# Moving the next page's transposes behind a page's first half of key products

## The chip, the cores and the metric

The kernel runs on one core of one Trainium2 chip. The metric is device microseconds of one launch, lower is better. Engines are named as in the profile: PE is TensorE, PEld its weight loads, DVE is VectorE, ACT is ScalarE, POOL is GpSimd, SP is SyncE.

## What is computed

One layer of a decoder for a prompt of 256 tokens and 8 sample sequences with a cache of 2048 positions each. Two branches (a gated delta rule and latent attention) share a normalised input, are merged by gates, and an MLP follows. The part at stake is the attention of the 8 samples over 16 cached pages each, 128 pages in all, every page 128 positions of 512 latent and 64 rope values:

```python
def mla_keys(latent, w_uk, w_uv, k_norm_nope):
    c = latent[..., :KV_LORA].astype(w_uk.dtype)
    kr = latent[..., KV_LORA:].astype(w_uk.dtype)
    kn = rms_norm((c @ w_uk).reshape(bsz, s, MLA_HEADS, NOPE_DIM), k_norm_nope)
    ...
def page_block(phys):
    kn, kr, v = mla_keys(cache_l[phys], w_uk, w_uv, k_norm_nope)
    return partial_softmax(mla_scores(qn, qr, kn, kr), v)
```

The kernel needs the product `c @ w_uk` (128 x 512 by 512 x 1024) of each page only for its sums of squares, that is for the norm of each head's key. The scores themselves come from queries that were multiplied into the latent space beforehand, four pages at a time.

## The kernel before, in words

The program has three stages: projections of prompt and sample (to about 209 us in the trace), a loop over the 128 pages (209 to 1350 us), and the gates and the MLP. All instructions are placed by hand, engine by engine; engines meet at semaphores only, and each runs its list in order. There is no scheduler.

In the loop, page n belongs to group g = n // 4 at position t = n % 4. The steps, by the names of the code:

- `transposes(n)` (PE, L1765): four 128x128 transposes of the page in `craw` into one bank of PSUM. `turned_page(n)` (ACT) copies that to `cTr` (L673) and rounds it to `cTh` (L676). `split_lo(n)` (DVE, L1079) writes the rest, `cTl = cTr - cTh`.
- `keys(n, half)` (PE, L1774 to L1776): twelve matmuls of 512 columns for each half of the key columns; it waits for `cTl` of its page. `squares(n, half)` (ACT, L682) squares the result, `norms(n, half)` (DVE, L1083) sums it by head.
- `query_products(g)` (PE, L1793 and L1795) at t = 3, `score_rows` (ACT, L692), `score_columns` (PE, L1801), `score_parts` (DVE, L1087), `maxima(g - 1)` (DVE, L1101 and L1103), `exps(g - 1)` (ACT, L698, writes `pst`), and on the next page, t = 0, `weigh(g - 2)` (PE, L1809, reads `pst`), `latent_rows` (ACT, L704), `latent_columns` (PE, L1815). At t = 2 `rope_columns` (PE, L1784) and `turned_rope` (ACT, L687). At t = 1 the DVE adds up scores and values of earlier groups.
- `beside(i)` on each engine: the delta rule runs as side work, pair of heads by pair of heads, in slots. Slot i = 2n stands before `keys(n, 0)`, slot 2n + 1 before `keys(n, 1)`. A pair takes 52 steps, k = 0 to 51, and the four pairs fill slots 6 to 213; the slots after them are empty. A step's PE part writes a bank, its DVE or ACT part reads it, and the PE part of the next step often waits for that.

Steps of the side work that the prediction names: k = 21 (ACT square root with a table load, L757), k = 22 (DVE Newton step), k = 27 (DVE writes `T_`, L1258 and L1260) and k = 28 (PE reads it, L1918), k = 49 (ACT square root with a table load, L779), k = 50 (DVE Newton step from L1175 to L1179), k = 51 (PE, L1835, reads its result).

The order on each engine within page n is before: PE `query_products` or `weigh`, `transposes(n + 1)`, `beside(2n)`, `keys(n, 0)`, the columns of that t, `beside(2n + 1)`, `keys(n, 1)`; ACT `latent_rows` or `score_rows`, `turned_page(n + 1)`, `beside(2n)`, `squares(n, 0)`, `turned_rope` or `exps`, `beside(2n + 1)`, `squares(n, 1)`; DVE `beside(2n)`, `split_lo(n + 1)`, `norms(n, 0)`, the sums of that t, `beside(2n + 1)`, `norms(n, 1)`.

Of the kernel before, what the change touches and what calls it, by code (L numbers as in the profile page):

```python
# [36 lines left out]
NT = NS * PAGES  # L37
# [101 lines left out]
def pair_slot(i):  # L139

    k = i - B_START
    return divmod(k, B_SLOTS) if 0 <= k < HP * B_SLOTS else (None, None)
# [11 lines left out]
def build(nc, I, O):  # L154
    C_in, ctx = I["consts"], ExitStack()
    with ctx:
        sems = {}

        def S(name):
            if name not in sems:  # L160
                sems[name] = ctx.enter_context(nc.semaphore(name))
            return sems[name]
# [234 lines left out]
        def wait(eng, name, value):  # L397

            if not isinstance(value, int) or value > 0:
                eng.wait_ge(S(name), value)  # L400
# [179 lines left out]
        def _(act):  # L580
# [97 lines left out]
            def squares(n, half_):  # L678
                k = 2 * n + half_
                act.wait_ge(S("half_done"), k + 1)  # L680
                wait(act, "kss_done", k - 1)
                nc.scalar.activation(ksq[:, half_], ps[:, k % 3, :], ACT.Square).then_inc(S("ksq_ready"), 1)  # L682

            def turned_rope(gg):
                act.wait_ge(S("rope_done"), gg + 1)
                wait(act, "qk_done", gg)
                nc.scalar.activation(rpT[:], ps[0:64, B_SUM, :], ACT.Copy).then_inc(S("rope_ready"), 1)  # L687

            def score_rows(gg):
                act.wait_ge(S("qk_done"), gg + 1)  # L690
                wait(act, "pvt_done", gg - 1)
                nc.scalar.activation(prows[:], ps[:, B_SCORE, :], ACT.Copy).then_inc(S("ssb_ready"), 1)  # L692
# [88 lines left out]
            def z_high(i):  # L781
                ns = NP + i
                act.wait_ge(S(f"z_landed{i % 2}"), 16 * (i // 2 + 1))
                if i >= 2:
                    act.wait_ge(S("chunk_done"), 4 * (ns - 1))
                nc.scalar.activation(wh2[:, ns % 2], wraw2[:, i % 2], ACT.Copy).then_inc(S("w_hi"), 1)

            def beside(i):
                b, k = pair_slot(i)
                if i < B_START:  # L790
                    decay_steps(i)
                elif b is not None:
                    pair_act(b, k)
                elif i == 2 * NT - 20:
                    z_high(0)
                elif i == 2 * NT - 16:
                    z_high(1)

            turned_page(0)
            for n in range(NT):  # L800
                g, t = n // 4, n % 4
                if t == 0 and g >= 2:
                    latent_rows(g - 2)
                if t == 3:
                    score_rows(g)
                if n + 1 < NT:
                    turned_page(n + 1)
                beside(2 * n)
                squares(n, 0)
                if t == 2:  # L810
                    turned_rope(g)
                if t == 3 and g >= 1:
                    exps(g - 1)
                beside(2 * n + 1)
                squares(n, 1)
# [62 lines left out]
        def _(v):  # L878
# [202 lines left out]
            def norms(n, half_):  # L1081
                v.wait_ge(S("ksq_ready"), 2 * n + half_ + 1)
                V.tensor_reduce(kss[:, n // 4 % 2, n % 4, 4 * half_:4 * half_ + 4], ksq[:, half_].rearrange("p (h d) -> p h d", h=4), AX, ALU.add).then_inc(S("kss_done"), 1)  # L1083
# [267 lines left out]
            def beside(i):  # L1351
                b, k = pair_slot(i)
                if i < B_START:
                    decay_steps(i)
                elif b is not None:
                    pair_dve(b, k)
                elif i == 2 * NT - 18:
                    z_low(0)
                elif i == 2 * NT - 14:
                    z_low(1)  # L1360

            split_lo(0)
            for n in range(NT):
                g, t = n // 4, n % 4
                beside(2 * n)
                if n + 1 < NT:
                    split_lo(n + 1)
                norms(n, 0)
                if t == 1 and g >= 1:
                    scaled(g - 1)  # L1370
                if t == 1 and g >= 2:
                    probabilities(g - 2)
                    latent_sum(g - 2)
                if t == 3:
                    score_parts(g)
                if t == 3 and g >= 1:
                    maxima(g - 1)
                beside(2 * n + 1)
                norms(n, 1)
                if t == 3:  # L1380
                    v.wait_ge(S("kss_done"), 2 * n + 2)
                    V.tensor_scalar(kss[:, g % 2], kss[:, g % 2], 1.0 / 128, EPS, ALU.mult, ALU.add).then_inc(S("ms_ready"), 1)  # L1382
# [154 lines left out]
            for g in range(2):  # L1537
                for u in range(8):
                    n = 8 * g + u + 2
# [13 lines left out]
        def _(pe):  # L1553
# [207 lines left out]
            def transposes(n):  # L1761
                pe.wait_ge(S(f"pages_landed{n // 4 % 3}"), 64 * (n // RING) + 64)
                wait(pe, "ct_raw", n)
                for c in range(4):
                    k = nc.tensor.transpose(trp[:, c, :], craw[:, n % RING, P * c:P * c + P], ident)  # L1765
                k.then_inc(S("tr_done"), 1)
# [31 lines left out]
            def score_columns(gg):  # L1798
                pe.wait_ge(S("ssb_ready"), gg + 1)
                for t in range(4):  # L1800
                    k = nc.tensor.transpose(stp[:, t, :], prows[:, P * t:P * t + P], ident)  # L1801
                k.then_inc(S("st_done"), 1)
# [180 lines left out]
            def beside(i):  # L1983
                b, k = pair_slot(i)
                if i == 5:
                    pe.wait_ge(S("g_ready"), 1)
                    pe.wait_ge(S("beta_ready"), 1)
                    p_ = begin_a("bg")
                    for n in range(2):
                        j = nc.tensor.transpose(p_[:, 64 * n:64 * n + 64], rw[:, CH * n:CH * n + CH], ident[0:64, 0:64])  # L1990
                    a_done(j)
                if b is not None:
                    pair_pe(b, k)

            transposes(0)
            for n in range(NT):
                g, t = n // 4, n % 4
                if t == 3:
                    query_products(g)
                if t == 0 and g >= 2:  # L2000
                    weigh(g - 2)
                if n + 1 < NT:
                    transposes(n + 1)
                beside(2 * n)
                keys(n, 0)
                if t == 0 and g >= 2:
                    latent_columns(g - 2)
                if t == 2:
                    rope_columns(g)
                if t == 3:  # L2010
                    score_columns(g)
                beside(2 * n + 1)
                keys(n, 1)

# [135 lines left out]
```

## Time and profile before

| | us |
|---|---|
| median of 3 runs | 1740.8 (1740.1 to 1743.41) |
| the profiled execution, its own time | 1745.99 |
| its span, first to last instruction | 1744.2 |
| PE busy in the span | 1674.2 |
| DVE busy | 898.7 |
| ACT busy | 638.4 |

The profiled execution is one run; its own time is 1.8 us above its span and 5.2 us above the median. PE is the engine that is nearly always busy, and its clock is granted in full in nearly all of the loop. A row of the trace reads: start in us from the span's start, length in us, engine, line, operation, names written and read; an idle stretch before it and what ended it stand in brackets.

### The profile page before, as it was taken

What the parts mean: (1) busy time and instruction counts of PE and PEld (TensorE: products, weight loads), DVE (VectorE), ACT (ScalarE), POOL (GpSimd) and SP (SyncE); (2) the same over time, 40 slices, a digit from 0 to 9 for tenths busy, and PEclk for the clock granted to TensorE, in tenths of its full rate; (3) what the DMA queues carried; (4) which work ended last, traced back from release to release, by engine and by line L of the source; (5) the groups of instructions that cost most, each with busy time, mean ns of one, the idle gap of its engine ahead of it and who ended that gap; (6) DMA issues with size and microseconds to landing.
All of it is one profiled execution on the core that took longest, in us unless ns stands there. A gap on an engine that the chain in (4) does not pass through costs nothing.

```text
span 1744.2 us, 26102 instructions
## 1 busy us (share of the span) xinstructions
PE 1674.2 (96%) x10164; PEld 1371.4 (79%) x10164; DVE 898.7 (52%) x1650; ACT 638.4 (37%) x954; POOL 213.5 (12%) x111
## 2 busy tenths in 40 slices
PE   6889899999999999999999999999999878999998
PEld 5865788687787787787877787876777778999998
DVE  5865444544455545455444555444333344677733
ACT  3221244533344433445333335234353323334431
POOL 0020011112111111211111211112121100000000
PEclk9995799999999999999999999999999988999999
DMA  7301132111232101331102310003110524555551
GB/s 241 97 1 55 50 82 64 40 29 39 73 88 65 28 28 30 96 87 53 28 28 57 103 41 28 28 28 115 43 55 1 175 91 169 170 169 176 186 177 66
DMA packets 110916, 138.68 MB, mean 80 GB/s; under 512 B 13584, under 2 KB 60208, under 8 KB 110664
## 3 DMA queue, kind: packets, MB, share of 16 engines
q1 hardware_dynamic: 106022, 134.43, 25.1%
q10 hardware_dynamic: 4602, 2.05, 0.5%
q8 instruction: 79, 1.29, 0.3%
q0 software_dynamic: 176, 0.61, 0.1%
q14 instruction: 37, 0.30, 0.1%
HBM read 130.52 MB, written 6.74 MB: 79 GB/s over the span
## 4 chain that ended last, share of the span: by engine, by line
PE 88%; DVE 7%; issue 2%; ACT 1%; ACTq 1%; POOL 0%; DVEq 0%; POOLq 0%
PE ps L1774 14%; PE ps L1776 13%; PE ps L1775 13%; PE ps L2070 5%; PE ps L2071 5%; PE ps L2072 5%; PE ps L1765 4%; PE ps L1793 2%; PE ps L1809 2%; PE ps L1860 1%; PE ps L1859 1%; PE ps L1861 1%; PE ps L1835 1%; PE ps L1926 1%; PE ps L1918 1%
## 5 line engine op out<-in xcount | busy, mean ns | idle before, releaser
L1774 PE MATMUL ps<-ukh,cTh 128*128 128x512 f32 x1024 | 425.7, 416 | 0.3 <-DVE cTl L1079 0.3
L1083 DVE TENSOR_REDUCE kss<-ksq 128x4 f32<-128x512 f32 x256 | 175.4, 685 | 447.8 <-ACT ksq L682 447.1
L1776 PE MATMUL ps<-ukh,cTl 128*128 128x512 f32 x1024 | 404.7, 395 | 0.0
L1775 PE MATMUL ps<-ukl,cTh 128*128 128x512 f32 x1024 | 404.0, 395 | 0.0
L682 ACT ACTIVATE ksq<-ps 128x512 f32<-128x512 f32 x256 | 152.7, 596 | 565.1 <-PE ps L1776 565.0
L1774 PEld LDWEIGHTS ps<-ukh,cTh 128*128 128x128 f32 x1024 | 194.7, 190 | 58.9 <-issue 24.2
L571 POOL TENSOR_TENSOR rk<-kss,mhalf 128x32 f32<-128x32 f32 x32 | 178.8, 5587 | 507.1 <-DVE kss L1382 507.1
L1776 PEld LDWEIGHTS ps<-ukh,cTl 128*128 128x128 f32 x1024 | 194.5, 190 | 44.9
L1775 PEld LDWEIGHTS ps<-ukl,cTh 128*128 128x128 f32 x1024 | 195.2, 191 | 33.8
L1425 DVE TENSOR_TENSOR wl<-wraw,wh 128x2048 fp32r<-128x2048 f32 x44 | 100.7, 2290 | 70.5 <-ACT wh L839 69.9
L839 ACT ACTIVATE wh<-wraw 128x2048 fp32r<-128x2048 f32 x44 | 84.3, 1916 | 137.9 <-PE ps L2072 125.5
L1079 DVE TENSOR_TENSOR cTl<-cTr,cTh 128x512 fp32r<-128x512 f32 x128 | 87.8, 686 | 27.1 <-ACT cTh L676 26.6
L2070 PE MATMUL ps<-Ah,wh 128*128 128x264 f32 x320 | 91.1, 285 | 1.6 <-DVE wl L1425 1.6
L1765 PEld LDWEIGHTS ps<-consts_sb,craw 128*128 128x128 f32 x512 | 59.4, 141 | 41.8 <-issue 33.5
L2072 PE MATMUL ps<-Ah,wl 128*128 128x264 f32 x320 | 90.8, 284 | 0.0
L2071 PE MATMUL ps<-Al,wh 128*128 128x264 f32 x320 | 90.7, 283 | 0.0
L673 ACT ACTIVATE cTr<-ps 128x512 f32<-128x512 f32 x128 | 76.2, 595 | 21.6 <-PE ps L1765 21.6
L676 ACT ACTIVATE cTh<-cTr 128x512 fp32r<-128x512 f32 x128 | 80.9, 632 | 4.1
L1765 PE MATMUL ps<-consts_sb,craw 128*128 128x128 f32 x512 | 81.0, 281 | 1.2 <-ACT cTr L673 0.9
L2027 PE MATMUL ps<-Ah,wh 128*128 128x264 f32 x192 | 60.2, 314 | 16.1 <-DVE zl L1344 14.1
L2072 PE MATMUL ps<-Hh,wl 128*128 128x264 f32 x256 | 72.9, 285 | 0.0
L2070 PE MATMUL ps<-Hh,wh 128*128 128x264 f32 x256 | 72.8, 284 | 0.0
(429 smaller groups left out, 2981.9 us busy)
## 6 DMA issues: line engine op xcount, KB each, us to landing
craw<-cache_mla SPq DMA_DIRECT2D x128, 288.0 KB, 3.2
wraw<-w_in SPq DMA_DIRECT2D x16, 1024.0 KB, 5.5
wraw<-w_up SPq DMA_DIRECT2D x16, 1024.0 KB, 5.4
wraw<-w_down SPq DMA_DIRECT2D x16, 1024.0 KB, 5.0
braw<-w_in SPq DMA_DIRECT2D x24, 512.0 KB, 3.9
sst<-state_gdn SPq DMA_DIRECT2D x32, 128.0 KB, 3.6
gdn_sample<-sst SPq DMA_DIRECT2D x32, 128.0 KB, 2.1
wraw<-w_ya SPq DMA_DIRECT2D x4, 1024.0 KB, 5.7
```

Source lines behind the costliest of these rows:

```text
L571: nc.gpsimd.tensor_tensor(rk[:, y], kss[:, y], mhalf[:], ALU.pow).then_inc(S("rk_ready"), 1)
L682: nc.scalar.activation(ksq[:, half_], ps[:, k % 3, :], ACT.Square).then_inc(S("ksq_ready"), 1)
L1079: V.tensor_tensor(cTl[:, n % 2], cTr[:, :, tokens(n)], cTh[:, n % 2].bitcast(F32), ALU.subtract).then_inc(S("ct_lo"), 1)
L1083: V.tensor_reduce(kss[:, n // 4 % 2, n % 4, 4 * half_:4 * half_ + 4], ksq[:, half_].rearrange("p (h d) -> p h d", h=4), AX, ALU.add).then_ ...
L1425: V.tensor_tensor(wl2[:, ns % 2], wraw2[:, (ns - NM) % 4], wh2[:, ns % 2].bitcast(F32), ALU.subtract).then_inc(S("w_lo"), 1)
L1765: k = nc.tensor.transpose(trp[:, c, :], craw[:, n % RING, P * c:P * c + P], ident)
L1774: mm(out, cTh[:, n % 2, c], ukh[:, c, cols], start=c == 0, stop=False)
L1775: mm(out, cTh[:, n % 2, c], ukl[:, c, cols], start=False, stop=False)
L1776: i = mm(out, cTl[:, n % 2, c], ukh[:, c, cols], start=False, stop=c == 3)
L2070: mm(out, w_hi, mh[:, kc, :], start=first and kc == 0, stop=False)
L2071: mm(out, w_hi, ml[:, kc, :], start=False, stop=False)
L2072: k = mm(out, w_lo, mh[:, kc, :], start=False, stop=last and kc == 3)
```

## The change

It moves three calls, one on each of three engines, and nothing else. The transposes of page n + 1 stood ahead of page n's first half of key products and now stand behind them, after the columns of that t and ahead of slot 2n + 1. ACT's copy and rounding stood ahead of slot 2n and now stand behind the squares of the first half. DVE's subtraction changes places with the sums of the first half. The number of instructions is the same; SP and POOL keep their lists.

```diff
@@ ACT
                 if t == 3:
                     score_rows(g)
+                beside(2 * n)
+                squares(n, 0)
                 if n + 1 < NT:
                     turned_page(n + 1)
-                beside(2 * n)
-                squares(n, 0)
                 if t == 2:
                     turned_rope(g)
@@ DVE
                 beside(2 * n)
+                norms(n, 0)
                 if n + 1 < NT:
                     split_lo(n + 1)
-                norms(n, 0)
                 if t == 1 and g >= 1:
                     scaled(g - 1)
@@ PE
                 if t == 0 and g >= 2:
                     weigh(g - 2)
-                if n + 1 < NT:
-                    transposes(n + 1)
                 beside(2 * n)
                 keys(n, 0)
...
                 if t == 3:
                     score_columns(g)
+                if n + 1 < NT:
+                    transposes(n + 1)
                 beside(2 * n + 1)
                 keys(n, 1)
```

Three places show the orders. The first is PE over the end of page 27 (t = 3) and the start of page 28 (t = 0), before; the key products between are left out.

```order
L1801 MATMUL ps<-consts_sb,prows 128x128 [waits ssb_ready]
L1801 MATMUL ps<-consts_sb,prows 128x128 x3
...
L1809 MATMUL ps<-craw,pst 32x512 [waits accT_ready,s_parts,pst_ready]
L1809 MATMUL ps<-craw,pst 32x512 x3
L1765 MATMUL ps<-consts_sb,craw 128x128 [waits ct_raw,pages_landed1]
L1765 MATMUL ps<-consts_sb,craw 128x128 x3
```

And with the change:

```order
L1801 MATMUL ps<-consts_sb,prows 128x128 [waits ssb_ready]
L1801 MATMUL ps<-consts_sb,prows 128x128 x3
L1765 MATMUL ps<-consts_sb,craw 128x128 [waits ct_raw,pages_landed1]
L1765 MATMUL ps<-consts_sb,craw 128x128 x3
...
L1809 MATMUL ps<-craw,pst 32x512 [waits accT_ready,s_parts,pst_ready]
L1809 MATMUL ps<-craw,pst 32x512 x3
```

The four transposes (L1765) of page 28 now follow the score columns in the middle of page 27, and those of page 29 no longer follow `weigh`.

The second is ACT on page 27, whose odd slot is step k = 49; L682 are the squares of the first and the second half, L698 writes `pst`. Before:

```order
L692 ACTIVATE prows<-ps 128x512 [waits pvt_done,qk_done]
L673 ACTIVATE cTr<-ps 128x4x128 [waits qk_done,tr_done]
L676 ACTIVATE cTh<-cTr 128x512 [waits half_done,ct_raw]
L682 ACTIVATE ksq<-ps 128x512 [waits kss_done,half_done]
L698 ACTIVATE pst<-ssc 128x4x8 [waits lall_done,pv_used,sub_ready]
L779 ACT_TABLE_LOAD
L779 ACTIVATE lr<-lr 2x264 [waits a_read]
```

And with the change:

```order
L692 ACTIVATE prows<-ps 128x512 [waits pvt_done,qk_done]
L682 ACTIVATE ksq<-ps 128x512 [waits kss_done,half_done]
L673 ACTIVATE cTr<-ps 128x4x128 [waits qk_done,tr_done]
L676 ACTIVATE cTh<-cTr 128x512 [waits half_done,ct_raw]
L698 ACTIVATE pst<-ssc 128x4x8 [waits lall_done,pv_used,sub_ready]
L779 ACT_TABLE_LOAD
L779 ACTIVATE lr<-lr 2x264 [waits a_read]
```

The copy and the rounding now stand between the first half's squares and `pst`.

The third is DVE on the same page. Before:

```order
L1079 TENSOR_TENSOR cTl<-cTr,cTh 128x512 [waits half_done,ct_hi]
L1083 TENSOR_REDUCE kss<-ksq 128x4 [waits ksq_ready]
L1087 TENSOR_REDUCE sparts<-ps 128x64 [waits st_done]
L1101 TENSOR_REDUCE mall<-smax 128x8 [waits smax_ready]
L1103 TENSOR_TENSOR ssc<-ssc,mall 128x32 [waits mall_ready]
```

And with the change:

```order
L1083 TENSOR_REDUCE kss<-ksq 128x4 [waits ksq_ready]
L1079 TENSOR_TENSOR cTl<-cTr,cTh 128x512 [waits half_done,ct_hi]
L1087 TENSOR_REDUCE sparts<-ps 128x64 [waits st_done]
L1101 TENSOR_REDUCE mall<-smax 128x8 [waits smax_ready]
L1103 TENSOR_TENSOR ssc<-ssc,mall 128x32 [waits mall_ready]
```

The score sums and the subtraction of the maximum, which `pst` waits for, now stand behind `cTl`, and `cTl` behind the first half's sums.

## Rows read from the trace of the kernel before

**Rows 1.** The page: busy us, share of the span and instructions of each engine

```profile
PE 1674.2 (96%) x10164; PEld 1371.4 (79%) x10164; DVE 898.7 (52%) x1650; ACT 638.4 (37%) x954; POOL 213.5 (12%) x111
```

**Rows 2.** PE's waits: line waited for, us in total, times, longest us

```profile
PE ps L1835 <- DVE lr L1179: 5.5, 8, 1.1
```

**Rows 3.** Timeline, PE and PEld, a page without side work, transposes between key products

```profile
1284.16 0.39 PE L1776 MATMUL ps<-ukh,cTl 128*128 128x512 f32 x1
1284.39 0.60 PE L1765 MATMUL ps<-consts_sb,craw 128*128 128x128 f32 x4
...
1287.15 0.19 PEld L1776 LDWEIGHTS ps<-ukh,cTl 128*128 128x128 f32 x1
1287.38 0.39 PE L1776 MATMUL ps<-ukh,cTl 128*128 128x512 f32 x1
```

**Rows 4.** Timeline, PE, ends of key products around query products and transposes

```profile
1262.83 0.39 PE L1776 MATMUL ps<-ukh,cTl 128*128 128x512 f32 x1
...
1265.20 0.40 PE L1775 MATMUL ps<-ukl,cTh 128*128 128x512 f32 x1
```

**Rows 5.** Timeline, PE, the same place on the last page, which has no transposes

```profile
1346.13 0.39 PE L1776 MATMUL ps<-ukh,cTl 128*128 128x512 f32 x1
...
1348.11 0.39 PE L1775 MATMUL ps<-ukl,cTh 128*128 128x512 f32 x1
```

**Rows 6.** Timeline, PE, two groups of four transposes in a row (page 8)

```profile
284.26 0.60 PE L1815 MATMUL ps<-consts_sb,prows 128*128 128x128 f32 x4
284.70 0.60 PE L1874 MATMUL ps<-consts_sb,tail 128*11 128x128 f32 x4
```

**Rows 7.** Timeline, ACT, squares, copy and rounding back to back

```profile
254.12 0.60 ACT L682 ACTIVATE ksq<-ps 128x512 f32<-128x512 f32 x1 [1.63 <-PE ps L1776]
254.62 0.59 ACT L673 ACTIVATE cTr<-ps 128x512 f32<-128x512 f32 x1
255.24 0.63 ACT L676 ACTIVATE cTh<-cTr 128x512 fp32r<-128x512 f32 x1
```

**Rows 8.** Timeline, DVE, one cTl, which waited for the rounding

```profile
1266.46 0.69 DVE L1079 TENSOR_TENSOR cTl<-cTr,cTh 128x512 fp32r<-128x512 f32 x1 [1.89 <-ACT cTh L676]
```

**Rows 9.** Timeline, t = 3 to t = 0: last key product, squares, score sums, pst, weigh

```profile
1267.48 0.39 PE L1776 MATMUL ps<-ukh,cTl 128*128 128x512 f32 x1
...
1267.91 0.60 ACT L682 ACTIVATE ksq<-ps 128x512 f32<-128x512 f32 x1 [1.48 <-PE ps L1776]
...
1268.54 0.69 DVE L1083 TENSOR_REDUCE kss<-ksq 128x4 f32<-128x512 f32 x1 [1.39 <-ACT ksq L682]
...
1269.14 0.41 DVE L1087 TENSOR_REDUCE sparts<-ps 128x64 f32<-128x256 f32 x1
...
1269.93 0.23 ACT L698 ACTIVATE pst<-ssc 128x32 f32<-128x32 f32 x1 [1.43 <-DVE ssc L1103]
...
1271.01 1.06 PE L1809 MATMUL ps<-craw,pst 128*32 128x512 f32 x8
```

**Rows 10.** Timeline, pages 27 and 28, side steps k = 49 to 51

```profile
462.63 0.60 ACT L682 ACTIVATE ksq<-ps 128x512 f32<-128x512 f32 x1 [2.68 <-PE ps L1776]
...
464.65 0.23 ACT L698 ACTIVATE pst<-ssc 128x32 f32<-128x32 f32 x1 [1.42 <-DVE ssc L1103]
464.89 1.28 ACT L779 ACT_TABLE_LOAD   x1
...
466.52 0.57 ACT L682 ACTIVATE ksq<-ps 128x512 f32<-128x512 f32 x1
...
467.94 1.78 DVE L1175 RECIPROCAL lr<-lr 2x264 f32<-2x264 f32 x1
...
471.46 1.15 PE L1835 MATMUL ps<-lr,consts_sb 2*128 2x264 f32 x4 [0.90 <-DVE lr L1179]
```

**Rows 11.** Windows of 10 us: busy us of PE, PEld, DVE, ACT, POOL, granted clock, DMA share, GB/s

```profile
472.00:482.00 10.00, 10.00 (x51) 8.35 (x50) 3.28 (x8) 2.78 (x4) 1.60 (x1) 0.83 0.15 46
...
610.00:620.00 10.00, 10.00 (x53) 7.51 (x52) 3.74 (x9) 2.78 (x5) 0.00 (x0) 0.83 0.00 0
```

## The prediction

> **What bounds the kernel now.** I read the page first: PE is busy for 96% of the span and no other engine for more than 52% [rows 1]. So PE's list, and the few places where PE waits, set the time. PE's waits come next. Inside the page loop there is one that counts: L1835 waits eight times, 5.5 us together, for DVE's Newton step of the side work [rows 2]. Everything else that ACT and DVE do for a page is done well before PE asks for it. The change takes no PE work away. It can gain only by a shorter stretch of PE or a shorter one of those eight waits, and it loses wherever the later place of a step makes it the last to arrive. So I went through PE's stretches, and then through every chain that ends at PE.
>
> **PE's own work.** Four transposes between key products take 0.44 us from start to start when other transposes stand before them [rows 6]. Behind query products they cost less: from the last key product before to the second one after it is 2.37 us with transposes [rows 4] and 1.98 us without [rows 5], so 0.39 us. Before, 31 of the 127 in the loop stand behind query products (t = 3) and 30 behind `weigh` (t = 0); I give `weigh`, for which no row without transposes exists, the same 0.39. Afterwards all stand between key products or behind transposes. That is 61 x 0.05 = 3.1 us more. Behind `weigh` the loss may be nothing (0.44 there too) or, as far on the other side, 0.1 each: 1.6 to 4.6 us in all. Page 1's transposes stood in PE's idle time while the very first `cTl` was made and come out of it: 0.4 us more. In pages t = 1 and t = 2 the 0.44 stays 0.44.
>
> **The chain to the next page's keys.** I put zero at the start of the last key product of a first half. Before, the chain from transposes to `cTl` had a whole page of time, afterwards one half. Squares start at 0.43 [rows 9], the copy 0.50 later, the rounding 0.62 after that for 0.63 us [rows 7], `cTl` 0.04 after its end (the gap from key product to squares [rows 9]) for 0.69 us [rows 8]: it starts at 2.22 and ends at 2.91. The transposes themselves end at 0.83 (0.23 to their start, 0.60 long) and don't delay the copy. The second half's last key product starts at 3.22 [rows 3], the next page's first 0.23 later, and its weights are loaded 0.23 ahead of it, at 3.22 again [rows 3]. So in the tightest page, t = 1, `cTl` is 0.31 us early at the load. At t = 0, 2 and 3 four more transposes stand in front: they end at 1.27, `cTl` starts at 2.59 and ends at 3.28, the load is at 3.66, 0.38 us early. No PE wait here, by the rows. The Trainium skill (TensorE: Matmul & The Clock Gate, "What happens when you issue a matmul") says that PE pulls weight loads ahead of running matmuls; the row of 0.23 us agrees. Counted to the matmul, as if nothing were pulled ahead, the margin would be 0.54 us and a wait here hardly possible. The sum is the same either way.
>
> **The chain to `weigh`.** At t = 3 the score sums (L1087) used to follow the first half's sums; they now stand behind `cTl`, which waits for ACT's rounding. An instruction that depends on nothing new starts 0.60 after the one before it (kss to sparts) [rows 9]. So L1087 starts at 2.59 + 0.60 = 3.19, before at 1.66. From it to `pst` is 0.79, and `pst` takes 0.23 [rows 9]: it ends at 4.21 and PE sees it at 4.25 (0.04, as from key product to squares). `weigh` stood at 3.53 [rows 9] and would now start 0.44 later, at 3.97. Before, `pst` was 0.85 us early. Now PE waits 0.28 us, unless the odd slot of that page puts PE work in between. It is empty at k = 5, 13 and 49 (groups 6, 7, 8, 19, 20, 21) and after the side work (groups 26 to 30), 11 groups. Two of them (k = 49) belong to the next paragraph. 9 x 0.28 = 2.5, and k = 17, whose two short transposes cover all but 0.06, adds 0.1: 2.6 us. With 0.1 us of doubt in each 0.28 that is 1.7 to 3.5.
>
> **The long wait, made longer.** Pages 27 and 79 (t = 3, k = 49) put a table load and a square root on ACT behind `pst` and ahead of the second half's squares. PE's L1835 on page 28 started 9.26 after the zero at 462.20 [rows 10] (the squares at 462.63, less 0.43). Now `pst` starts at 3.98, the table load 0.24 later, squares 1.63 after that, the reciprocal 1.42 later, L1835 another 3.52 [rows 10]: 10.79. The zero itself comes 0.39 earlier, so 10.40 against 9.26: 1.14 us more, twice, 2.3 us. The other two pairs have k = 49 at t = 1, where only the 1.16 us (2.22 + 0.60 less 1.66) by which everything behind `cTl` starts later, and ACT's part of it, count: about 0.2 each. k = 21 at t = 3 on ACT delays the other Newton step by as much, twice: 0.8 us together.
>
> **The other side steps.** Walking k = 0 to 51 with each step's start 1.2 to 1.6 us later in odd slots, one more is late: k = 27 at t = 0. `T_` starts at 3.19 and needs two DVE operations the size of `cTl`, 1.4 us, so 4.6. PE gets to L1918 at 3.22 + 0.44 + 0.44 + 0.23 = 4.33: 0.3 us, for two of four pairs, 0.6 us. At t = 2 query products cover it. Even slots of ACT now stand ahead of the copy, but each of them is through by the end of the first half, apart from k = 18, and that delay is covered by the work of slot k = 19. The eight waits of rows 2 do not shrink: the PE work up to them is the same, only in another order.
>
> **The clock.** After the pause at L1835 in rows 10 the granted clock falls: 0.83 in the next 10 us [rows 11], so 3.4 us at 1.2 instead of 2.4 GHz, 1.7 us lost. Such a fall followed one of the eight waits. A wait of 2 us instead of 0.9 makes one more likely in the pair whose clock stayed up so far. I count one: 1.7 us.
>
> **Sum.** 3.1 + 0.4 + 2.6 + 2.3 + 0.8 + 0.6 + 1.7 = 11.5 us. On the profiled execution's own 1745.99 us that gives 1757.5. The median of the runs lies 5.2 us lower, so 1752.3, and I say 1752.
>
> **Rivals.**
> 1. No change that can be measured. A measurement of this kernel can tell about 0.2%, 3.5 us, from nothing. If the semaphore and queue times are a little shorter than I read them, the waits of 0.3 us vanish and the one at L1835 lies under another; the arrangement of PE alone costs 1.6 to 3.5 us: 1743. For it: none of the small waits is larger than 0.3 us. Against it: the 1.14 us at k = 49 is read off one dependent chain.
> 2. Faster. The granted clock falls four times in the loop, once after rows 10 and three times at the 32 tiny products of k = 28 (L1934), one of them in the second window of [rows 11] at 0.83 again, 1.7 us each. Before, transposes stood just ahead of that stretch, now key products do. If those three falls go and rival 1 holds as well, it is 1740.8 + 2.5 - 5.1 = 1738.2. It decides at two falls fewer. Against it: the stretch of tiny products itself is as long as before.
> 3. Slower than forecast. The 0.31 and 0.38 us of margin at t = 1 and t = 0 are the place. If each handover costs 0.1 us more than in the rows (there are five in the chain), PE waits 0.1 to 0.2 us in 63 pages, 6 to 13 us more: 1758 to 1765. By the margin of 0.54 above this would not happen. It decides at 0.06 us per handover.
>
> **Chances and range.** Forecast 0.62, rival 1 0.17, rival 2 0.05, rival 3 0.16. The forecast's own range is 1745 to 1757: arrangement 1.6 to 4.6, waits 0.9 less or more, clock none to three falls. To hold 8 in 10 it takes in the upper part of rival 1 and the lower of rival 3: 1743 to 1762. Faster by over 0.2% 0.04, within 0.2% 0.15, slower 0.81.
>
> **What would show it.** In the profile after: L1809 waiting for `pst` about eleven times at 0.2 to 0.4 us (before: never in the loop); the longest wait of L1835 near 2 us at pages 28 and 80; L1918 waiting twice for `T_`; L1774 hardly waiting for `cTl`. From the last key product before query products to the second after it 1.98 us instead of 2.37. If L1774 waits for `cTl` in dozens of pages, rival 3 holds. If L1809 never waits, my reading of the handovers is wrong. If PE's busy time and waits add up as before and the time still falls, it is the clock.

## The result: 0.67% slower, and where the time went

| | before | after |
|---|---|---|
| median, us | 1740.74 (1740.1 to 1743.41) | 1752.89 (1751.68 to 1754.44) |
| ratio | | 1.0067, 95% interval 1.005 to 1.0085 |
| the profiled execution, its own time | 1745.99 | 1752.75 |
| its span | 1744.2 | 1750.9 |
| first key product of the loop to the last | 1140.2 | 1152.2 |

The forecast of 1752 was met within 1 us, and the time is clearly longer than before. The sizes of two terms behind the forecast were not met, as shown below. Both columns rest on four runs. Beside the later experiments the kernel before was run 64 more times, with medians of 1742.4, 1743.4 and 1743.1 us, and the kernel after was not run again, so the loss may be nearer to 10 us than to 12. The loop alone is 12.0 us longer, the medians differ by 12.15 us. The two spans differ by less, 6.7 us, because the stages outside the loop, which the change doesn't touch, took 5.3 us longer in the profiled execution of before. That is also about how far that execution lay above its median.

The page of after first: its busy times, which answer to [rows 1], and PE's granted clock by slices.

```profile
PE 1674.8 (96%) x10164; PEld 1376.4 (79%) x10164; DVE 901.7 (51%) x1650; ACT 644.8 (37%) x954; POOL 214.2 (12%) x111
...
PEclk9995799999999999999999999999999988999999
```

PE is busy 1674.8 us, before 1674.2 [rows 1]: as much work in a longer span. The slices are too coarse for single clock falls. So the next view is PE's waits in after (engine, line, what it waited for: us in all, times, longest). They answer to [rows 2].

```profile
PE ps L1835 <- DVE lr L1179: 7.8, 8, 1.6
...
PE ps L1809 <- ACT pst L698: 5.9, 12, 2.7
...
PE ps L1774 <- DVE cTl L1079: 2.2, 1, 2.2
...
PE ps L1918 <- DVE T_ L1260: 0.4, 2, 0.2
```

L1835 went from 5.5 to 7.8 us. L1809 waits twelve times: the one of 2.7 us is at 1387 us, behind the loop, where the wait stood before too (3.2 us), and the other eleven, inside the loop, are new. L1774 waits once, for the very first page. L1918 is new. Inside the loop the waits grew from 5.5 us to 7.8 + 3.2 + 0.4 = 11.4 us, by 5.9 us.

In the two profiled executions the clock makes up most of the rest. I read it in windows of 10 us from 229 to 1349 us and summed twice the missing share of each, since a missing half is the level of 1.2 instead of 2.4 GHz: PE spent 17.0 us of the loop at 1.2 GHz before, 27.2 us after. Work done at half speed costs half its time, so that is 10.2 / 2 = 5.1 us more at most. The windows behind the two long waits show it, columns as in [rows 11]. First after:

```profile
470.00:480.00 10.00, 8.40 (x41) 6.97 (x41) 4.18 (x9) 1.82 (x3) 3.80 (x1) 0.83 0.27 89
...
960.00:970.00 10.00, 8.36 (x31) 6.17 (x30) 6.14 (x11) 2.35 (x5) 5.49 (x1) 0.76 0.44 125
965.00:975.00 10.00, 10.00 (x42) 8.12 (x41) 2.49 (x5) 0.96 (x2) 1.56 (x1) 0.66 0.08 27
```

and the second of these stretches before:

```profile
960.00:970.00 10.00, 9.10 (x55) 7.66 (x54) 5.00 (x12) 3.28 (x5) 3.63 (x1) 1.00 0.31 96
```

The fall behind the first long wait was there before [rows 11], the one behind the second (page 80) is new. One more is new, at 364 us, 1 us behind the end of the 32 tiny products of k = 28 (L1934), which run from 359.6 to 363.2 us.

**The waits one by one.** PE at the start of page 28 in after (start, length, engine, line, operation, and the idle time before it with its cause):

```profile
464.46 0.39 PE L1776 MATMUL ps<-ukh,cTl 128*128 128x512 f32 x1
465.13 1.06 PE L1809 MATMUL ps<-craw,pst 128*32 128x512 f32 x8 [0.28 <-ACT pst L698]
...
469.03 0.60 PE L1815 MATMUL ps<-consts_sb,prows 128*128 128x128 f32 x4
469.46 0.60 PE L1765 MATMUL ps<-consts_sb,craw 128*128 128x128 f32 x4
471.66 1.15 PE L1835 MATMUL ps<-lr,consts_sb 2*128 2x264 f32 x4 [1.60 <-DVE lr L1179]
```

The pause ahead of L1835 was 0.90 us before [rows 10] and is 1.60 now, and 0.28 more are lost ahead of L1809. At page 80 it is 0.90 to 1.64, and 0.29. ACT and DVE over the same stretch, in after:

```profile
461.27 0.60 ACT L682 ACTIVATE ksq<-ps 128x512 f32<-128x512 f32 x1 [3.31 <-PE ps L1776]
462.15 0.60 ACT L673 ACTIVATE cTr<-ps 128x512 f32<-128x512 f32 x1 [0.28 <-PE ps L1765]
462.78 0.63 ACT L676 ACTIVATE cTh<-cTr 128x512 fp32r<-128x512 f32 x1
464.85 0.23 ACT L698 ACTIVATE pst<-ssc 128x32 f32<-128x32 f32 x1 [1.44 <-DVE ssc L1103]
465.10 1.28 ACT L779 ACT_TABLE_LOAD   x1
...
466.72 0.57 ACT L682 ACTIVATE ksq<-ps 128x512 f32<-128x512 f32 x1
```

```profile
461.91 0.69 DVE L1083 TENSOR_REDUCE kss<-ksq 128x4 f32<-128x512 f32 x1 [3.16 <-ACT ksq L682]
463.44 0.69 DVE L1079 TENSOR_TENSOR cTl<-cTr,cTh 128x512 fp32r<-128x512 f32 x1 [0.85 <-ACT cTh L676]
464.05 0.42 DVE L1087 TENSOR_REDUCE sparts<-ps 128x64 f32<-128x256 f32 x1
...
468.14 1.78 DVE L1175 RECIPROCAL lr<-lr 2x264 f32<-2x264 f32 x1
```

DVE sits idle for 0.85 us ahead of `cTl`, since ACT's rounding isn't through, and the score sums (L1087), whose input is there by then, stand in its list behind `cTl`. From there the delay runs through `pst`, the table load, the squares and the reciprocal to L1835.

### The profile page after: what moved, and what is told of

The parts are those of the page before. It is cut to its first block, busy times and chain, and to the rows that moved or that the text cites. A ratio compares the mean times of both kernels' runs of the same rounds, so it can differ in the third digit from the quotient of the medians.

```text
span 1750.9 us, 26110 instructions
## 1 busy us (share of the span) xinstructions
PE 1674.8 (96%) x10164; PEld 1376.4 (79%) x10164; DVE 901.7 (51%) x1650; ACT 644.8 (37%) x954; POOL 214.2 (12%) x111
## 4 chain that ended last, share of the span: by engine, by line
PE 85%; DVE 8%; ACT 3%; issue 2%; ACTq 1%; POOL 0%; DVEq 0%; POOLq 0%
PE ps L1774 13%; PE ps L1776 12%; PE ps L1775 12%; PE ps L2070 5%; PE ps L2071 5%; PE ps L2072 5%; PE ps L1765 3%; PE ps L1793 2%; PE ps L1809 2%; PE ps L1859 1%; PE ps L1918 1%; PE ps L1860 1%; PE ps L1861 1%; PE ps L1926 1%; PE ps L1835 1%
## 5 line engine op out<-in xcount | busy, mean ns | idle before, releaser
L1774 PE MATMUL ps<-ukh,cTh 128*128 128x512 f32 x1024 | 425.0, 415 | 2.2 <-DVE cTl L1079 2.2
L1083 DVE TENSOR_REDUCE kss<-ksq 128x4 f32<-128x512 f32 x256 | 175.4, 685 | 427.6 <-ACT ksq L682 427.5
L682 ACT ACTIVATE ksq<-ps 128x512 f32<-128x512 f32 x256 | 152.7, 597 | 538.5 <-PE ps L1776 538.4
L1774 PEld LDWEIGHTS ps<-ukh,cTh 128*128 128x128 f32 x1024 | 195.2, 191 | 75.7 <-issue 37.9
L1765 PE MATMUL ps<-consts_sb,craw 128*128 128x128 f32 x512 | 77.5, 274 | 0.4 <-issue 0.4
L2071 PE MATMUL ps<-Hl,wh 128*128 128x264 f32 x256 | 72.8, 284 | 0.0
```

The source lines that it names most:

```text
L1774: mm(out, cTh[:, n % 2, c], ukh[:, c, cols], start=c == 0, stop=False)
L2071: mm(out, w_hi, ml[:, kc, :], start=False, stop=False)
```

## The experiments

The theory, W: the loss is the waits that the late `cTl` makes at t = 3, through L1087 and `pst`, with the clock falls that follow, and PE's own order costs little. Against it A: the arrangement of PE's list costs the time. And C: the clock alone, wherever it falls. The ratios below are to the kernel before in the runs made beside each experiment: median 1742.4 us for the first two sections and for `act_dve_only`, 1743.4 for `pe_only`, `delay2`, `newton_before` and `newton_scores_after`, 1743.1 for `delay1` and `newton_after`. They are taken over all runs and can differ a little from the ratio of the medians. The diffs below are against the kernel before.

### The change on one part of the pages

`t3_only` makes the change on the 32 pages with t = 3 alone, on all three engines. `not_t3` makes it on the 96 others. The diff is of PE; ACT and DVE have the same conditions.

```diff
-                if n + 1 < NT:
+                if n + 1 < NT and not (t == 3):
                     transposes(n + 1)
                 beside(2 * n)
                 keys(n, 0)
...
+                if n + 1 < NT and t == 3:
+                    transposes(n + 1)
                 beside(2 * n + 1)
```

> The change is made on the 32 pages with t = 3 only; the other 96 keep the old order on all three engines. Theory W (the loss is the score chain that now ends behind cTl, and the table load of k = 49 behind it, both at t = 3 only): PE waits at L1809 eleven times at 0.29 us, L1835 waits 1.6 instead of 0.9 at pages 28 and 80, and most of the 12.1 us stays: 1748 to 1751 us. Rival R (each of the 127 moved groups of transposes costs a little, by a thinner margin for cTl or by its place on PE): a quarter of the loss, about 1743.8 us. Rival C (the clock alone, at chance): anything, with L1809 not waiting.

> The change is made on the 96 pages with t = 0, 1 and 2 only. Theory W: L1809 never waits, L1918 waits twice for T_ at 0.2 us, two of the eight L1835 waits are 0.2 us longer: 1741.5 to 1744 us, the upper end if the fall of the clock at page 17 is there. Rival R: three quarters of the loss, about 1749.8 us.

Measured: `t3_only` 1747.84 us, 1.0039 of before (1.0022 to 1.0057); `not_t3` 1743.06 us, 1.0008 (0.9989 to 1.0027). The waits of `t3_only`, in which `weigh` is L1813 and the products of the Newton step L1839:

```profile
PE ps L1839 <- DVE lr L1181: 7.4, 8, 1.7
...
PE ps L1813 <- ACT pst L698: 5.6, 12, 2.6
```

All eleven waits for `pst` (5.6 less 2.6 for the one behind the loop) and most of the growth of the Newton waits come with the quarter of the pages that have t = 3. The other three quarters cost nothing that this measurement can tell, though its interval reaches 0.27%. The time of `t3_only` is 5.4 us over the before beside it, 0.39 of the 0.67%: more than the 0.17% that a quarter of the loss would be, but less than the 7 to 10 us I had expected. The two parts add up to 0.47%; where the rest belongs their intervals can't tell. W's place is right.

### The score sums ahead of the subtraction

`scores_first` keeps the change in full, but at t = 3 DVE does `score_parts` and `maxima` before `split_lo`, instead of behind it:

```diff
                 beside(2 * n)
+                norms(n, 0)
+                if t == 3:
+                    score_parts(g)
+                if t == 3 and g >= 1:
+                    maxima(g - 1)
                 if n + 1 < NT:
                     split_lo(n + 1)
-                norms(n, 0)
...
-                if t == 3:
-                    score_parts(g)
-                if t == 3 and g >= 1:
-                    maxima(g - 1)
```

> The change in full, but at t = 3 DVE takes the score sums and the maxima ahead of cTl instead of behind it. Theory W: pst ends 0.6 to 1.3 us earlier, L1809 doesn't wait (3.2 us back), the squares behind the table load of k = 49 are on time and L1835 waits about 1.0 instead of 1.6 there (1.2 us back, and with it a fall of the clock, 1.7 us): 1745 to 1748 us. Rival R: as with the change, 1752 to 1753 us.

Measured: 1742.12 us, 0.9999 (0.9986 to 1.0012). The whole loss is gone, more than I had expected. Its waits (one of the four for `pst`, 2.8 us, is the one behind the loop, the other three are of 0.16 us):

```profile
PE ps L1835 <- DVE lr L1179: 4.4, 6, 1.4
...
PE ps L1809 <- ACT pst L698: 3.3, 4, 2.8
```

DVE at a page with t = 3 late in the loop of `scores_first`, and the `weigh` that follows on PE with its neighbours:

```profile
1318.50 0.69 DVE L1083 TENSOR_REDUCE kss<-ksq 128x4 f32<-128x512 f32 x1 [3.59 <-ACT ksq L682]
1319.10 0.42 DVE L1087 TENSOR_REDUCE sparts<-ps 128x64 f32<-128x256 f32 x1
...
1320.03 0.69 DVE L1079 TENSOR_TENSOR cTl<-cTr,cTh 128x512 fp32r<-128x512 f32 x1 [0.17 <-ACT cTh L676]
```

```profile
1321.05 0.39 PE L1776 MATMUL ps<-ukh,cTl 128*128 128x512 f32 x1
1321.37 1.06 PE L1809 MATMUL ps<-craw,pst 128*32 128x512 f32 x8
1322.37 0.50 PE L1774 MATMUL ps<-ukh,cTh 128*128 128x512 f32 x1
1322.70 0.39 PE L1775 MATMUL ps<-ukl,cTh 128*128 128x512 f32 x1
```

and a like page of after, where `weigh` waits:

```profile
1334.57 0.39 PE L1776 MATMUL ps<-ukh,cTl 128*128 128x512 f32 x1
1335.25 1.07 PE L1809 MATMUL ps<-craw,pst 128*32 128x512 f32 x8 [0.29 <-ACT pst L698]
1336.24 0.50 PE L1774 MATMUL ps<-ukh,cTh 128*128 128x512 f32 x1
1336.59 0.40 PE L1775 MATMUL ps<-ukl,cTh 128*128 128x512 f32 x1
```

The sums fill the time in which DVE would wait for the rounding, and `cTl` starts 0.93 us behind L1087 with little idle time of its own. At this page `weigh` no longer waits. From the key product before it to the second one behind it is 1.65 us, in after 2.02: a wait shown as 0.29 us made the stretch 0.37 longer. A itself falls here: PE has the same order as in after, and ACT too, and no loss is left that the interval of 0.13% would show. It is more than a loss undone in every place, though. At pages 28 and 80 L1835 waits 0.43 and 0.45 us, before 0.90, and this and two short waits which are gone (0.31 each) pay for three new waits of 0.16 for `pst`, two of 0.19 at L1918, and two waits of L1835 that grew from 1.14 to 1.36.

### ACT and DVE alone, and PE alone

`act_dve_only` moves `turned_page` on ACT and `split_lo` on DVE as the change does, and leaves PE's transposes where they stood. `pe_only` does the opposite half. On ACT, in `act_dve_only` (DVE as in the change):

```diff
-                if n + 1 < NT:
-                    turned_page(n + 1)
                 beside(2 * n)
                 squares(n, 0)
+                if n + 1 < NT:
+                    turned_page(n + 1)
```

On PE, in `pe_only`:

```diff
-                if n + 1 < NT:
-                    transposes(n + 1)
                 beside(2 * n)
                 keys(n, 0)
...
                 if t == 3:
                     score_columns(g)
+                if n + 1 < NT:
+                    transposes(n + 1)
```

> Only ACT's copy and rounding and DVE's cTl are moved; PE's transposes stay at the start of the page. Theory W: at t = 3 cTl starts at 2.22 instead of 2.59 after the last key product but weigh is due at 3.53 instead of 3.97, so L1809 waits a little longer, 0.35 us eleven times: 1748 to 1752 us, with at most 1 to 3 us for the place of the transposes missing. Rival R in the form that the transposes' place on PE costs the time: 1741 us, as before.

> Only PE's transposes are moved; ACT still has copy and rounding ahead of slot 2n and of the first half's squares, and so has to wait for the transposes behind the first half before it does either. Theory W: cTl ends at 2.84 instead of 2.91, but squares and the even slot's work on ACT are 1.7 us late and more; L1809 waits about 0.4 us and the side work waits in many even slots: 1755 to 1775 us. Rival R: 1752 us, all of the loss and no more.

Measured: `act_dve_only` 1751.17 us, 1.0051 (1.0035 to 1.0067); `pe_only` 1803.75 us, 1.0346 (1.0325 to 1.0367). The waits of `act_dve_only` first, then those of `pe_only`:

```profile
PE ps L1835 <- DVE lr L1179: 8.6, 8, 1.8
PE ps L1809 <- ACT pst L698: 6.0, 12, 2.7
```

```profile
PE ps L1809 <- ACT pst L698: 21.0, 17, 2.7
PE ps L1835 <- DVE lr L1179: 14.4, 8, 2.7
```

The waits of after are there without one transpose moved, and three quarters of the loss with them (0.51 of 0.67%; the intervals overlap). With only the transposes moved, in `pe_only`, ACT's copy stands ahead of the first half's squares and waits for transposes that come behind that half. Everything behind it on ACT is late by a half page, and the time is beyond my 1755 to 1775. The range was missed in size: PE waits 42.3 us longer in the loop, 18.4 us of it at `weigh`, and the clock costs 17.1 (table below). So the moves on ACT and DVE must go with the one on PE, and it is they that carry its price.

### A delay by itself

These two move nothing. At t = 3 DVE repeats the first half's sum (L1083), once in `delay1` and twice in `delay2`, ahead of the real one; `link` makes each wait for the end of the one before it. L1087 and all behind it come 0.7 and 1.4 us later; the change itself made it 1.5 us later from the zero of the prediction (3.2 instead of 1.7), but with `weigh` 0.4 later too.

```diff
                 if n + 1 < NT:
                     split_lo(n + 1)
+                if t == 3:
+                    v.wait_ge(S("ksq_ready"), 2 * n + 1)
+                    for _ in range(2):
+                        link(V.tensor_reduce(kss[:, n // 4 % 2, n % 4, 0:4], ksq[:, 0].rearrange("p (h d) -> p h d", h=4), AX, ALU.add))
                 norms(n, 0)
```

> Nothing is moved. In the kernel before, at t = 3 only, DVE sums the first half's squares three times instead of once (the two extra sums give the same values), which delays the score sums, pst and what stands behind pst on ACT by about 1.44 us (two dependent operations of 0.72), and leaves transposes and cTl where they were. Theory W: pst is seen at 3.93 after the last key product, weigh is due at 3.53, so L1809 waits 0.4 us eleven times (4.4 us), L1835 waits 1.4 us more at pages 28 and 80 (2.9 us, less 0.8 that L1809 has taken), and the clock falls there once more (1.7 us): 8 us in all, 1748 to 1752 us when before is at 1742. Rival R (the transposes' place): as before, 1742 us.

> As delay2, with one extra sum instead of two: the score chain at t = 3 ends 0.73 us later than before (two of them turned a lead of 0.85 us into a wait of 0.62 us). Theory W, with a point from which it decides: pst is still 0.12 us early, L1809 doesn't wait at all, and only the two L1835 waits at pages 28 and 80 grow by 0.7 us each, with one more fall of the clock: 1 to 4 us over before. Rival (every delay of the score chain costs in proportion): half of what delay2 cost, 8 us over before.

Measured: `delay2` 1760.08 us, 1.0097 (1.0078 to 1.0116), more than expected; `delay1` 1745.83 us, 1.0015 (1.0 to 1.0031), 2.7 us over before and as expected, and under the 8 us that a cost in proportion would be. PE's waits for `pst` in `delay2`, then in `delay1`:

```profile
PE ps L1813 <- ACT pst L698: 10.0, 14, 3.0
```

```profile
PE ps L1813 <- ACT pst L698: 2.6, 1, 2.6
```

In `delay1` `weigh` doesn't wait inside the loop (the 2.6 us are the wait behind it), and only L1839 does, 7.1 us in all and 1.63 at both long places: the table load and the Newton step come behind `pst`, and the pause takes over its delay in full (0.90 + 0.73). In `delay2`, at a page with t = 3 and the `weigh` behind it:

```profile
1333.21 0.39 PE L1780 MATMUL ps<-ukh,cTl 128*128 128x512 f32 x1
...
1336.31 0.41 DVE L1087 TENSOR_REDUCE sparts<-ps 128x64 f32<-128x256 f32 x1
...
1337.10 0.23 ACT L698 ACTIVATE pst<-ssc 128x32 f32<-128x32 f32 x1 [2.87 <-DVE ssc L1103]
1337.38 1.07 PE L1813 MATMUL ps<-craw,pst 128*32 128x512 f32 x8 [0.57 <-ACT pst L698]
```

`weigh` starts 0.05 us behind the end of `pst` and 4.17 behind the last key product of the first half, where before it started at 3.53 with `pst` ended at 2.68 [rows 9]. The margin was 3.53 - 2.68 - 0.05 = 0.80 us. Delays of L1087 by 0.72 us (`delay1`), 1.16 (`act_dve_only`) and 1.44 (`delay2`) made `weigh` later by nothing, 0.37 and 0.64: each time the excess over 0.80. The rows show 0.07 less, 0.30 and 0.57. I had put 0.4 for the last one because I left out the 0.23 us of `pst` itself. `delay2` cost twice what I had expected since the waits for `pst` are thirteen (two of 0.35 at k = 17) and 7.0 us in place of 4.4, and since its clock fell more often (below). With nothing else changed, a delay of L1087 makes the waits of the change, larger ones and two more, in the same places.

### The Newton step one slot earlier

The eight waits for DVE's Newton step, 5.5 us before [rows 2], stand in every kernel so far, though not always all eight. `newton_before` is the kernel before with the Newton steps at the end of slots k = 21 and k = 49 instead of k = 22 and k = 50. `newton_after` is the change with the same edit, `newton_scores_after` is `scores_first` with it.

```diff
-                if k == 22:
+                if k == 21:
                     newton(4, 2 * b + 1, consts[0:4, C_RSQ], "row_rstd")
...
-                if k == 50:
+                if k == 49:
                     newton(2, 2 * b + 2, 1.0, "row_rstd")
```

> The kernel before with DVE's Newton step moved from the start of k = 22 and k = 50 to the end of k = 21 and k = 49, 1.3 to 2.9 us earlier. Theory: the eight waits at L1835 (5.5 us) are what is left of PE's waits in the loop; they go, and with the one at page 28 a fall of the clock (1.7 us): 1735 to 1738 us when before is at 1742. Rival: the Newton step now delays the second half's sums and the side work behind it, and the waits only change their place: 1741 to 1743 us.

> The change, the score sums ahead of cTl as in the run scores_first, and the Newton step early as in newton_before. Theory: the same 5 to 7 us come off as from the kernel before, 1735 to 1738 us; the place of the transposes is worth nothing either way. Rival: the later start of ACT's square root (behind the rounding) holds the Newton step, and DVE waits for it ahead of the second half's sums: 1739 to 1743 us.

> The change in full, with the Newton step early as in newton_before, and the score sums where the change has them, behind cTl. Theory W: L1809 waits 0.29 us eleven times as with the change (3.2 us), L1835 hardly waits, so 3 to 4 us over newton_scores_after's place and 8 to 10 us under the change: 0.1 to 0.3% over before. Rival: at pages 27 and 79 the square root comes 1.5 us later and DVE now holds the second half's sums for it, so most of the L1835 wait comes back: 0.4 to 0.6% over before.

Measured: `newton_before` 1734.42 us, 0.9945 (0.9927 to 0.9963); `newton_scores_after` 1740.54 us, 0.9982 (0.9969 to 0.9994); `newton_after` 1743.51 us, 1.0003 (0.9988 to 1.0018). In `newton_before` L1835 doesn't wait at all. The windows behind pages 28 and 80 in it:

```profile
470.00:480.00 10.00, 10.00 (x58) 8.27 (x58) 4.06 (x9) 2.84 (x6) 5.85 (x1) 1.00 0.26 86
960.00:970.00 10.00, 10.00 (x55) 8.19 (x54) 5.57 (x14) 3.56 (x6) 0.24 (x2) 1.00 0.20 54
```

No pause, no fall there. It beats both kernels. With the Newton step early, the change still costs 0.6% against `newton_before`, by way of its other waits and the clock. `newton_after` keeps all eleven waits for `pst` (3.2 us) and 1.3 us at L1835. It came out at the lower end of what I had expected, 0.1 to 0.3% over before, and its rival, most of the wait at L1835 coming back, is out. So the longer wait at L1835 is one part of the loss, not its root. `newton_scores_after` gained less than the 5 to 8 us I had expected, and its time lies in the rival's 1739 to 1743. Of the rival's own cause, waits at L1835 that come back, only 0.6 us show. It keeps waits of 1.5 us (L1835 0.6, L1809 0.5, L1918 0.4), the 0.5 us of the first page, and 3.6 us more at the low clock than `newton_before`, which is 1.8 us. That sums to 3.8 us, as much as the loops of the two profiled executions differ by. The medians are 6 us apart; the profiled executions differ by another 2.5 outside the loop, where the two kernels are the same.

### One account for all kernels

For each profiled execution, against before: how much longer PE waits inside the loop (all waits from the second key product on), half the change in time at 1.2 GHz (17.0 us before), 0.5 us where page 1's transposes moved out of the idle start, and the sum, beside the measured change in the loop (first key product to last).

| kernel | waits | clock | first page | sum | loop |
|---|---|---|---|---|---|
| after | +5.9 | +5.1 | 0.5 | +11.5 | +12.0 |
| t3_only | +4.9 | +3.4 | | +8.3 | +9.2 |
| not_t3 | +0.1 | +6.8 | 0.5 | +7.4 | +7.2 |
| scores_first | -0.2 | 0.0 | 0.5 | +0.3 | +0.2 |
| act_dve_only | +6.4 | +1.7 | | +8.1 | +9.3 |
| pe_only | +42.3 | +17.1 | 0.5 | +59.9 | +61.4 |
| delay1 | +1.6 | -1.7 | | -0.1 | +0.1 |
| delay2 | +9.3 | +6.9 | | +16.2 | +16.7 |
| newton_before | -5.5 | -1.7 | | -7.2 | -7.5 |
| newton_scores_after | -4.0 | +0.1 | 0.5 | -3.4 | -3.7 |
| newton_after | -0.6 | +1.8 | 0.5 | +1.7 | +2.1 |

Waits and clock account for every kernel to 1.5 us with no term for the order of PE's list. Where eleven waits for `pst` are in, the sum is 0.4 to 1.2 us short; 11 x 0.08, the part of such a wait that its row doesn't show (0.37 against 0.29), is 0.9. The clock's column is of one execution of each kernel, so this shows where its time went, not what the kernel would lose to the clock every time.

Apart from `pe_only`, the clock's falls in the loop are of two kinds. Some follow a long wait of PE. At pages 28 and 80, with pauses of 1.6 to 1.7 us at L1835, it fell behind both in five kernels (after, `t3_only`, `delay1`, `delay2`, `act_dve_only`) but behind the first alone in `pe_only` (1.62 and 1.64); with 0.90 us (before) and 0.84 (`not_t3`) behind the first alone; with 0.45 or less (`scores_first`, the three Newton kernels) behind neither. At pages 54 and 106 there are pauses as long, and the clock mostly stays up: in `act_dve_only` they are 1.79 us each, in after and `scores_first` 1.36, before 1.14, and no fall follows any of these. In `pe_only` one follows the first of two of 1.8. `not_t3` fell behind one of its two of 1.36 (at 719 us), `delay2` behind one of its two of 1.14. Page 54 in `act_dve_only`, and the window behind the pause (columns as in [rows 11], the granted clock is the 1.00):

```profile
719.49 1.15 PE L1835 MATMUL ps<-lr,consts_sb 2*128 2x264 f32 x4 [1.79 <-DVE lr L1179]
```

```profile
719.00:729.00 10.00, 9.51 (x64) 7.11 (x65) 3.61 (x8) 2.21 (x5) 0.60 (x1) 1.00 0.01 2
```

So the length of the pause alone doesn't decide it; what else does, no run shows. The other falls come behind the tiny products of k = 28: for three of the four pairs before, in some kernels for all four, in `delay1` for two.

How much of this belongs to the kernel can be told in part from the granted clock of each run over its whole span, loop and the rest. In the 23 runs of before beside `delay1` the two with 0.959 took 1751.7 and 1752.0 us, and the 12 with 0.965 or 0.966 took 1739.5 to 1743.1: 0.006 of 1742 us is 10 us, so the spread of one kernel is mostly its clock. The mean is 0.9648 in the 24 runs of before beside the first experiments and 0.9633 in the four of after. My estimate from that, the difference times 1745 us, is that the change loses 2.7 us to the clock on average, not the 5.1 of the two profiled executions; the two sets were not run side by side, so this is rough. For `t3_only` (0.9644) it is 0.6 us, for `act_dve_only` (0.9642) 1.1, for `delay2` (0.9602 against 0.9646) 7.6, for `scores_first` (0.9650) and `delay1` (0.9643 against 0.9641) none. C by itself is out: after waits 5.9 us longer in the loop, and `delay1` has no more of the low clock than before while its long pauses grew as W says.

## Why the prediction was right, point by point

- **PE bound, its waits decide.** Right. PE's busy time is the same, and waits and clock make up the difference in every kernel.
- **PE's own order, 3.1 us.** Wrong: about nothing. The step that failed is "In pages t = 1 and t = 2 the 0.44 stays 0.44" together with reading the price only up to the second key product: the 0.44 us of [rows 6] is the distance between two sets of transposes and was taken for a set between key products too. Over a whole half, in pages 110 to 126 of the traces (each half from last key product to last key product), a set of four transposes alone between key products costs 0.49 to 0.50 us, joined to other transposes 0.40 to 0.41, behind `weigh` 0.37 and behind query products 0.39. Before, a group of four pages has 0.37 + 0.50 + 0.49 + 0.39 = 1.75 us; after, three sets are joined and one stands alone, 0.40 + 0.49 + 0.41 + 0.40 = 1.70. The gain is at t = 2, where the transposes now join the rope columns. By these pages PE's own work is 0.05 us shorter in a group, about 1.5 us in 32 groups, where I had put 3.1 us longer. The 1.98 us expected around query products without transposes is there (1.98 and 1.97).
- **First page, 0.4 us.** Measured 0.5.
- **The chain to the next page's `cTl`.** Right, no wait in 126 pages, the first one apart, though `cTl` is made a half page later. In after it starts 2.21 us and ends 2.90 behind the last key product of the first half at t = 1 (forecast 2.22 and 2.91), and at 2.60 and 3.29 in the other pages without side work (2.59 and 3.28). Page 125, its `cTl` and the next page's first key product:

```profile
1347.46 0.69 DVE L1079 TENSOR_TENSOR cTl<-cTr,cTh 128x512 fp32r<-128x512 f32 x1 [0.46 <-ACT cTh L676]
1348.69 0.39 PE L1774 MATMUL ps<-ukh,cTh 128*128 128x512 f32 x1
```

That is 0.54 us early, as forecast. Rival 3 is out. Its price was too high as well: of the 63 pages that it counted only 18 have a margin under 1 us, since in the others side work stands between.
- **The chain to `weigh`, 2.6 us.** Right in place, number and size: 11 waits of 0.28 or 0.29, in the eleven groups named, nine of which make 2.6 us. k = 17 didn't wait (0.1 expected). What the rows leave out is the 0.08 us each. The lead of 0.85 us was counted to the end of `pst`, without the 0.04 that I gave it afterwards; against 4.25 it is 0.81, and measured 0.80.
- **The long wait, 2.3 us.** Right in its chain: from `pst` to the table load 0.25, to the squares 1.62, to the reciprocal 1.42, to L1835 3.52, against 0.24, 1.63, 1.42 and 3.52. The loss at page 28 is 0.70 at L1835 and 0.28 at L1809, together 0.98, at page 80 0.74 + 0.29 = 1.03; forecast 1.14. The announced wait "near 2 us" was 1.6: I added the whole delay to 0.90 and forgot that L1809 takes 0.28 of it.
- **The other Newton waits, 0.8 us.** 0.22 more at 716 and at 1211 us, and as much at 583 and 1078 us (0.31 before, 0.50 and 0.53 after): 0.85.
- **k = 27, 0.6 us.** Two waits, as said, of 0.19 each: 0.4.
- **The clock, 1.7 us.** Under-sized: up to 5.1 in the profiled executions, 2.7 by the estimate from all runs. The new fall at page 80 is the one counted. The time at 1.2 GHz grew by 10.2 us: 3.4 us are the fall at 364 us, and the fall at page 80 lasts 6.8 us, twice as long as one of the prediction's falls (0.66 from 965 to 975 us alone). The prediction priced each of the four falls before at 1.7 us; the one at 852 us is 6.8 us long too (0.66 from 850 to 860 us). Rival 2 is out: no fall went, two came.

The sum, 11.5 against the 12.0 us of the profiled loops, came out since the arrangement was 3 us too high and the clock 3.4 us too low. The forecast's own range doesn't follow from its terms: 1.5 us of arrangement, 0.9 of waits and one fall fewer or two more give 1748 to 1758, not 1745 to 1757. The mechanism is shown: it comes and goes with the order on DVE at t = 3, and rival 1, in which the small waits vanish, is out with the eleven waits. The closeness of the number is in part luck.

## What to carry to other kernels

When a step moves in an engine's list, ask of everything that stands behind it whether it now waits for an input that it doesn't need; here a subtraction that waits for another engine held up score sums whose input was ready, and one reordering took the whole loss back. Price such a move by the margin of each step behind it: a delay under the margin of 0.80 us made no wait at `weigh`, and one beyond it made `weigh` later by as much as it exceeded it. And look where PE waits already before weighing an order of small gains: the waits at L1835 of 5.5 us could be taken away by moving the five instructions of the Newton step by one slot, worth 0.55%.

## What the runs showed of the hardware

- The cost of four 128x128 transposes depends on the neighbours: 0.49 to 0.50 us between products of 512 columns, 0.40 to 0.41 behind other transposes, 0.37 behind the `weigh` products, 0.39 behind query products. Their rows show 0.60 us from the first's start to the last's end, and 0.66 where they cost least.
- A wait of PE that the trace shows as 0.29 us made its stretch 0.37 us longer, and waits shown as 0.30 and 0.57 us made `weigh` 0.37 and 0.64 us later.
- Pauses of 1.6 to 1.7 us at pages 28 and 80 were followed by a fall of the granted clock at both places in each of five kernels, and at one of two in a sixth. Pauses of 1.79 us at pages 54 and 106 of `act_dve_only` were followed by none, and no fall came behind pauses of 0.45 us or less at L1835.
- The same kernel took 1740 us at a granted clock of 0.965 to 0.966 over its span and 1752 at 0.959.
- A DVE sum of 128x512 that waits for the end of the same sum before it starts 0.72 to 0.73 us behind that one's start, the next instruction, which doesn't wait for it, 0.60 us behind it.
